# Gate, up and first products of a feed-forward layer with the weights standing in the array and the activations moving

## The reference

```python
u = rms_norm(h, norm_mlp_pre[l])
f = jnp.square(jax.nn.relu(u @ w_mlp_in[l])) @ w_mlp_out[l]
h = h + rms_norm(f, norm_mlp_post[l])
...
def swiglu(h, w_in, w_out):
    gu = h @ w_in
    g, u = jnp.split(gu, 2, axis=-1)
    return (jax.nn.silu(g) * u) @ w_out
```

## Time and profile before

| what | value |
|---|---|
| median of 3 runs | 1351.31 us (1350.66 to 1353.59) |
| profiled execution, its time | 1354.33 us |
| span of that execution | 1352.2 us |
| TensorE busy | 1318.8 us, 98% |
| TensorE weight loads busy | 1086.1 us, 80% |
| VectorE busy | 927.8 us, 69% |
| ScalarE busy | 661.6 us, 49% |
| granted TensorE clock, mean | 0.996 |

### The profile page before, as it was taken

The page is one execution under the profiler, slowest core; times in us unless marked ns, Lnnn a source line. Parts: engine busy times, 40 slices in busy tenths (PEclk is TensorE's granted clock), DMA queues, the critical chain, the costliest instruction groups (busy, mean ns, idle before and its releaser), DMA issues.

```text
span 1352.2 us, 16396 instructions
## 1 busy us (share of the span) xinstructions
PE 1318.8 (98%) x6611; PEld 1086.1 (80%) x6611; DVE 927.8 (69%) x1023; ACT 661.6 (49%) x928; POOL 28.4 (2%) x56
## 2 busy tenths in 40 slices
PE   8999999999999999999999999999999999999998
PEld 8987577788887888888788888788888887788887
DVE  5277888775658776677876667966666786744444
ACT  5345865645456333335533335753334566644442
POOL 2200010000000000000000000000000000000000
PEclk9999999999999999999999999999999999999999
DMA  9997668877775677874677784597777633455551
GB/s 254 244 312 248 184 209 323 293 282 276 271 289 203 244 273 279 279 279 170 227 263 280 273 311 170 170 308 272 254 277 280 223 125 96 155 187 187 187 187 62
DMA packets 162762, 317.98 MB, mean 235 GB/s; under 512 B 7128, under 2 KB 108944, under 8 KB 153472
## 3 DMA queue, kind: packets, MB, share of 16 engines
q1 hardware_dynamic: 158800, 305.44, 65.9%
q0 software_dynamic: 3712, 11.45, 3.3%
q10 hardware_dynamic: 176, 0.05, 0.0%
HBM read 314.56 MB, written 1.84 MB: 234 GB/s over the span
## 4 chain that ended last, share of the span: by engine, by line
PE 85%; DVE 7%; ACT 4%; DMA 2%; issue 1%; ACTq 0%; SPq 0%; DVEq 0%
PE bank L733 26%; PE bank L735 26%; PE bank L734 26%; DMA raw<-in_w_in 2%; PE bank L831 2%; DVE full L1949 2%; PE bank L754 1%; ACT whi L1374 1%; DVE wlo L1853 1%; DVE xt L1937 1%; DVE mix L1935 1%; PE bank L781 1%; PE bank L1089 0%; PE bank L757 0%; ACT mix L1390 0%
## 5 line engine op out<-in xcount | busy, mean ns | idle before, releaser
L1853 DVE TENSOR_TENSOR wlo<-raw,whi 128x2048 fp32r<-128x2048 f32 x202 | 462.6, 2291 | 244.7 <-ACT whi L1374 244.5
L1374 ACT ACTIVATE whi<-raw 128x2048 fp32r<-128x2048 f32 x205 | 392.3, 1914 | 208.6 <-PE bank L735 174.8
L733 PE MATMUL bank<-whi,uhi 128*128 128x512 f32 (+2 forms) x1168 | 455.3, 390 | 7.8 <-DVE ulo L1962 5.1
L735 PE MATMUL bank<-whi,ulo 128*128 128x512 f32 (+2 forms) x1168 | 447.0, 383 | 0.0
L734 PE MATMUL bank<-wlo,uhi 128*128 128x512 f32 (+2 forms) x1168 | 445.6, 381 | 0.0
L733 PEld LDWEIGHTS bank<-whi,uhi 128*128 128x128 f32 x1168 | 220.6, 189 | 54.2 <-issue 12.6
L735 PEld LDWEIGHTS bank<-whi,ulo 128*128 128x128 f32 x1168 | 220.2, 188 | 43.6
L734 PEld LDWEIGHTS bank<-wlo,uhi 128*128 128x128 f32 x1168 | 220.9, 189 | 41.0 <-issue 0.5
L733 PE MATMUL bank<-whi,hsplit 128*128 128x512 f32 (+1 forms) x512 | 200.8, 392 | 0.0
L735 PE MATMUL bank<-whi,hsplit 128*128 128x512 f32 (+1 forms) x512 | 198.5, 388 | 0.0
L734 PE MATMUL bank<-wlo,hsplit 128*128 128x512 f32 (+1 forms) x512 | 198.3, 387 | 0.0
(11 more groups left out here) (263 smaller groups left out, 946.4 us busy)
## 6 DMA issues: line engine op xcount, KB each, us to landing
raw<-in_ffn_w_in SPq DMA_DIRECT2D x176, 512.0 KB, 4.9
ada<-in_ada_w SPq DMA_DIRECT2D x72, 1024.0 KB, 7.4
raw<-in_ffn_w_out SPq DMA_DIRECT2D x44, 1024.0 KB, 5.1
raw<-in_w_in SPq DMA_DIRECT2D x16, 1024.0 KB, 10.1
raw<-in_w_mlp_in SPq DMA_DIRECT2D x16, 1024.0 KB, 6.9
raw<-in_w_mlp_out SPq DMA_DIRECT2D x16, 1024.0 KB, 5.0
ada<-in_kv_ada_w SPq DMA_DIRECT2D x8, 1024.0 KB, 7.3
raw<-in_w_kv SPq DMA_DIRECT2D x8, 1024.0 KB, 5.2
```

The costliest lines, as they stand in the source:

```text
L733: nc.tensor.matmul(o, sh, mh, start=start, stop=False, skip_group_check=skip)
L735: return nc.tensor.matmul(o, sl, mh, start=False, stop=stop, skip_group_check=skip)
L1374: ins = nc.scalar.activation(whi[:, ring(n), :], raw[:, ring(n), :], ACT.Copy)
L1853: ins = nc.vector.tensor_tensor(wlo[:, ring(n), :], raw[:, ring(n), :], whi[:, ring(n), :].bitcast(F32), ALU.subtract)
```

## The change

In every chunk but a layer's first the two "g" slots are done by a new function, `hidden_slot`: blocks of the weights (128 x 128) are the stationary operand, and all 256 tokens of `u` move. The hidden values come out feature-major: gate in bank 4 and up in bank 5 for an `ffn`, four blocks of 128 columns in banks 4 and 5 for `mlp`. `hf5` and `hf2` then hold feature-major values, `h_high` and `h_low` read them from `mix` instead of bank 6, and `turn_h` remains only for the pieces of a layer's first chunk (two in `mlp`, one in each `ffn`; 6 of 60).

```diff
+        TURNED = {0: 1, 1: 2}
+        for name in ("ffn0", "ffn1", "ffn2", "ffn3"):
+            TURNED[PIECE0[name]] = len(TURNED) + 1
+        def h_of(p):
+            if p in TURNED:
+                return bank[6][:]
+            return mix[:, 512 * (p % 2):512 * (p % 2) + 512] if p < 2 * MLP_N else mix[:, 512:1024]
...
+            def hidden_slot(n, q):
+                pe.wait_ge(lo_done, n + 1)
+                wh, wl = v4(whi, n), v4(wlo, n)
+                for f in range(4):
+                    o = bank[4 + f // 2][:, (f % 2) * T:(f % 2 + 1) * T]
+                    m = slice(f * P, (f + 1) * P)
+                    for k in range(4):
+                        kk = 4 * q + k
+                        ins = mm3(o, wh[:, k, m], wl[:, k, m], uhi[:, kk, :], ulo[:, kk, :],
+                                  kk == 0 and f % 2 == 0, kk == KT - 1, skip=True)
+                ins.then_inc(pe_done, 1)
+                piece(n)
...
             for i in range(1, MLP_N):
-                u_slot(b + MLP_AT["g", i, 0], 0, o)
-                turn_h(2 * i - 2, i - 1, hf5, 0)
-                u_slot(b + MLP_AT["g", i, 1], 1, o)
-                turn_h(2 * i - 1, i - 1, hf5, 256)
+                hidden_slot(b + MLP_AT["g", i, 0], 0)
+                if i == 1:
+                    turn_h(0, 0, hf5, 0)
+                hidden_slot(b + MLP_AT["g", i, 1], 1)
+                if i == 1:
+                    turn_h(1, 0, hf5, 256)
                 down(b + MLP_AT["d", i - 1, 0], 2 * i - 2, first=i == 1)
-                if i == MLP_N - 1:
-                    turn_h(2 * i, i, hf5, 0)
                 down(b + MLP_AT["d", i - 1, 1], 2 * i - 1)
             i = MLP_N - 1
-            turn_h(2 * i + 1, i, hf5, 256)
...
                 for i in range(1, FFN_N):
-                    u_slot(b + FFN_AT["g", i, 0], 0, o)
+                    hidden_slot(b + FFN_AT["g", i, 0], 0)
-                    turn_h(p0 + i - 1, c0 + i - 1, hf2, 0)
-                    u_slot(b + FFN_AT["g", i, 1], 1, o)
+                    if i == 1:
+                        turn_h(p0, c0, hf2, 0)
+                    hidden_slot(b + FFN_AT["g", i, 1], 1)
...
-                down_wait(n, p0 + i - 1)
-                down_half(n, p0 + i - 1, 0, False)
-                turn_h(p0 + i, c0 + i, hf2, 0)
-                down_half(n, p0 + i - 1, 1, False).then_inc(pe_done, 1)
-                piece(n)
                 down_last(b + FFN_AT["d", i, 0], p0 + i)
...
             def take_hidden(i):
                 act.wait_ge(pe_done, START["mlp"] + MLP_AT["g", i, 1] + 1)
+                if i > 1:
+                    act.wait_ge(h_lo, 2 * i)
...
                         for t in range(2):
+                            if i > 1 and t == 0:
+                                dve.wait_ge(h_lo, p0 + i)
                             dve.wait_ge(g_act, g0 + 2 * i + t + 1)
```

More of the change, by code:

```diff
@@ L1171, in _ @@
             for i in range(1, MLP_N):
-                o = [hidden_bank("mlp", i, t) for t in range(2)]
                 if i == 1:
@@ L1201, in ffn @@
                 for i in range(1, FFN_N):
-                    o = [hidden_bank(name, i, t) for t in range(2)]
                     if i > 1:
@@ L1216, in ffn @@
                         pe.wait_ge(v2_taken, 4)
-                    if i < FFN_N - 1:
-                        down(n, p0 + i - 1, first=i == 1)
+                    down(n, p0 + i - 1, first=i == 1)
                 i = FFN_N - 1
-                down_wait(n, p0 + i - 1)
-                down_half(n, p0 + i - 1, 0, False)
-                turn_h(p0 + i, c0 + i, hf2, 0)
-                down_half(n, p0 + i - 1, 1, False).then_inc(pe_done, 1)
-                piece(n)
                 down_last(b + FFN_AT["d", i, 0], p0 + i)
@@ L1614, in h_high @@
             def h_high(p):
-                act.wait_ge(h_turned, p + 1)
+                if p in TURNED:
+                    act.wait_ge(h_turned, TURNED[p])
+                elif p < 2 * MLP_N:
+                    act.wait_ge(h_full, p + 1)
+                else:
+                    act.wait_ge(h_full, 2 * (p - MLP_N + 1))
                 if p >= 2:
                     act.wait_ge(pe_done, PIECE_SLOT[p - 2] + 1)
-                nc.scalar.activation(hb(p)[0], bank[6][:], ACT.Copy).then_inc(h_hi, 1)
+                nc.scalar.activation(hb(p)[0], h_of(p), ACT.Copy).then_inc(h_hi, 1)
             def take_hidden(i):
                 act.wait_ge(pe_done, START["mlp"] + MLP_AT["g", i, 1] + 1)
+                if i > 1:
+                    act.wait_ge(h_lo, 2 * i)
                 for t in range(2):
@@ L1647, in ffn @@
                         for t in range(2):
-                            nc.scalar.activation(act_g[:, t, :], hidden_bank(name, i, t)[:, 0:256],
-                                                 ACT.Silu).then_inc(g_act, 1)
+                            gate = bank[4][:, t * T:(t + 1) * T] if i else hidden_bank(name, i, t)[:, 0:256]
+                            nc.scalar.activation(act_g[:, t, :], gate, ACT.Silu).then_inc(g_act, 1)
+                        if i == FFN_N - 1:
+                            h_high(p0 + i)
                     conv(b + at + 3)
-                h_high(p0 + FFN_N - 1)
                 nc.scalar.preload_act_table_set(LN_EXP)
@@ L2222, in h_low @@
                 dve.wait_ge(h_hi, p + 1)
-                nc.vector.tensor_tensor(hb(p)[1], bank[6][:], hb(p)[0].bitcast(F32), ALU.subtract).then_inc(h_lo, 1)
+                nc.vector.tensor_tensor(hb(p)[1], h_of(p), hb(p)[0].bitcast(F32), ALU.subtract).then_inc(h_lo, 1)
             for at, (kind, i, q) in enumerate(MLP_ORDER[:-2]):
@@ L2252, in ffn @@
                         for t in range(2):
+                            if i > 1 and t == 0:
+                                dve.wait_ge(h_lo, p0 + i)
                             dve.wait_ge(g_act, g0 + 2 * i + t + 1)
-                            nc.vector.tensor_tensor(hf2[:, t, :], act_g[:, t, :], hidden_bank(name, i, t)[:, 256:512],
-                                                    ALU.mult).then_inc(h_full, 1)
+                            lin = bank[5][:, t * T:(t + 1) * T] if i else hidden_bank(name, i, t)[:, 256:512]
+                            nc.vector.tensor_tensor(hf2[:, t, :], act_g[:, t, :], lin, ALU.mult).then_inc(h_full, 1)
                         if i == FFN_N - 1:
```

## The result

Over 7 runs each, the changed kernel has a median of 1357.84 us (1356.08 to 1359.99) and the kernel before 1352.62 us (1350.66 to 1354.92). The ratio is 1.0035, with a 95% interval of 1.0024 to 1.0046, so by the ratio the change made the kernel 4.7 us slower (3.2 to 6.2); the two medians lie 5.2 us apart. 1354.5 was forecast against a median of 1351.31, a ratio of 1.0024.

What follows compares the result with a forecast made beforehand. The prediction took TensorE's own instructions to bound the layers, without idle time. Added slots at +28.2 us less removed pieces at 24.9 us gave +3.3 us on 1351.31, rounded down to 1354.5 us, range 1351.0 to 1359.0.

Steps and rivals of the forecast that it cites:

- The slot's price: 94 "g" slots with 48 matmuls of 256 columns for 24 of 512: 5.46 to 5.76 us each, +28.2 us.
- the two upper rows: Profile rows for a new "g" slot: 5.76 us from equal-form matmuls (taken), 5.83 from pooling, whose group changes cost extra.
- The pieces' price: 54 transposed pieces removed from `mlp` and `ffn` chunks, at 0.47, 0.43 or 0.45 us each: 24.9 us saved.
- The waits: Two new waits, for `h_low` in `mlp` and within VectorE in an `ffn`, end in time and cost nothing.
- the cover: Time to spare before TensorE would wait for hidden values: 3.2 us in an `ffn`, 11.2 us in `mlp`.
- Only columns cost: Rival: the 94 narrower-matmul slots add nothing, all 24.9 us of pieces are gained, time 1326.4 us; chance 0.03.
- The down slots get faster: Rival: pieces and bank 6 splits slow 60 down slots, so 7.2 us come back, time 1347.3 us; chance 0.08.
- the sum's size: Whole kernel: slots' +28.2 us less pieces' 24.9 us gives +3.3 us; this summed case had chance 0.79.

Runs made afterwards that it cites:

- the cut into 256 and 256: Kernel before with every 512-wide matmul of the 94 changed slots cut into two of 256 columns, transposes kept: ratio 1.0194, 26.2 us slower.
- without transposes: Changed kernel with the old 512-wide slots back under the new order and the transposes left out: ratio 0.983 against the kernel before, 23.0 us faster.

## Why the prediction was right

**The slot's price was right.** +0.30 us was forecast from the earlier trace rows, and 11.51 / 2 = 5.755 us against 5.455 was found, 28.2 us over 94 slots. The choice between the two upper rows was right as well: with four groups of twelve matmuls a slot, no group change cost anything.

**The pieces' price was right.** Middle chunks came out at 17.09 and 22.66 us where 17.11 and 22.7 stood. The 0.02 us less is mostly the down slot, 5.576 instead of 5.589 once it follows narrow matmuls. Without slots of the new kind, the pieces alone measured 25.9 us in the layers for 24.9 in the sum, which the prediction had called their upper bound.

**The waits were right.** The new wait of `take_hidden` for `h_lo` and the wait of the "g" slots for `h_full` show no idle time on TensorE, as the cover (3.2 us in an `ffn`, 11.2 in `mlp`) said.

**The rivals.** "Only columns cost" is refuted by the cut into 256 and 256. The formula of the Trainium skill (TensorE: Matmul & The Clock Gate, section "Back-to-back issue gap"), which the section gives for an isolated matmul, comes to 109 ns; the runs show 120 for matmuls with a weight load each. "The down slots get faster" saw a true oddity, 5.59 against 5.47, and gave a wrong cause: the change left it alone. Its price was near (7.2 forecast, 8.6 measured in the layers).

**What was less right is the sum's size against the measured time.** 3.3 us was forecast, the layers of the trace show 2.1, the span 2.8, and the ratio of the runs 4.7, with the lower end of the interval at 3.2. Of the 1.2 us that the layers are below the sum, the 0.02 us of each of 36 middle `ffn` chunks is 0.7.

What the ratio is above the layers, 2.6 us, is a term that the prediction put at nothing: the part of the program ahead of `mlp`, whose code is the same. That the total came out as near as it did owes something to luck, since this term and the shortfall of the layers have opposite signs. The term is not noise alone. By ratio less layers it is +2.6 us for the change, +3.6 for its `ffn` half and +2.9 without transposes, the three kernels that have the new order in the `ffn` layers; for the other eight kernels with several executions it lies between -2.2 and +1.0. In those three an execution also takes 2.3 us outside the span, in the kernel before and the one with `mlp` alone 2.1.

In the 14 traces of this study the first down matmul of `mlp` starts anywhere from 259.1 to 264.1 us after the start. Part of that scatter goes with the granted clock, which the prediction read as full in all 40 slices: a slice of 34 us still shows a 9 with 3.4 us of half clock in it. Three windows: up to the first down matmul of `mlp` in the kernel before, a stretch inside it with the clock down, and up to the same place with the change (busy time of PE, PEld, DVE, ACT, POOL, then clock, DMA, GB/s):

```profile
0.00:261.90 261.90, 244.63 (x1561) 203.23 (x1562) 188.04 (x326) 149.11 (x267) 23.58 (x47) 0.98 0.83 258
94.80:98.20 3.40, 3.40 (x13) 2.62 (x11) 3.40 (x2) 0.33 (x2) 0.00 (x0) 0.50 1.01 349
0.00:263.20 263.20, 244.91 (x1608) 204.76 (x1609) 187.96 (x326) 149.13 (x267) 23.54 (x47) 0.99 0.84 258
```

The trace of the kernel before has 10.2 us at half clock there, that of the change 6.8, the one that starts `mlp` last (264.1) 13.7, and the one that starts it first (259.1) none. But the changed kernel starts `mlp` 1.4 us later than the kernel before with less time at half clock, and only 0.60 of that is its chunk 1. So the clock does not explain the surplus of the change. Why the head is longer in kernels whose `ffn` layers differ, far behind it, stays open.

## What to carry to other kernels

Cost a matmul as its columns at the clock plus a price per matmul (here 13 ns), with a floor for narrow ones (here 0.11 us), and weigh a change of operand roles as added matmuls against removed transposes: here 24 more matmuls cost 0.30 us and one transposed piece 0.47, so it pays only where a slot rids the engine of more than 0.6 of a piece. Take the price from starts in the timeline, never from mean durations, which count the overlap. And where one product runs slower than another of the same shape, compare the addresses of its two operands before looking for contention.

## What the runs showed of the hardware

- With both operands at the same place within 512 bytes, a 512-wide fp32r matmul with its own weight load starts 0.2269 us after the last one, a 256-wide one 0.1199, both 13 ns over their columns at 2.4 GHz. A 192-wide one, in one execution, starts after 0.11, 30 ns over.
- At 256 columns it makes no difference which of the two operands is the weights: 5.75 us a slot either way.
- When stationary and moving operand start 128 bytes apart within 512, 512-wide matmuls are 0.2325 us apart; 192 bytes, 0.2289; at the same place, 0.2269. I had not expected any dependence on addresses. Other differences were not tried at this width, and other widths were not compared.
- A slot of matmuls behind four transposes of 128 columns takes longer, by 0.12 us with 24 wide ones (5.58 against 5.46) and by 0.09 with 48 narrow ones (5.84 against 5.75).
- Between 50 and 240 us into the span the granted clock was at half for 0 to 13.7 us, differently from trace to trace and for 3.4 or 6.8 us at a time; ahead of one such fall, at 94.8 us in the kernel before, TensorE had been busy for 3.45 of 4.8 us.
